# A hybrid layer: seven block products in two more phases of its first network, modulation weights in quarters, four modulation tiles on TensorE

## What is computed

```python
def swiglu(h, w_in, w_out):
    a, b = jnp.split(h @ w_in, 2, axis=-1)          # w_in 1024 x 5632
    return (jax.nn.silu(a) * b) @ w_out             # w_out 2816 x 1024

def trunk_layer(x, mod, n_pre, n_post, f_in, f_out, mix_w, ctx):
    sh0, sc0, g0, sh1, sc1, g1, sh2, sc2, g2 = jnp.split(mod, N_MOD, axis=-1)
    h = rms_norm(x, n_pre[0]) * (1 + sc0) + sh0
    x = x + 0.5 * g0 * rms_norm(swiglu(h, f_in[0], f_out[0]), n_post[0])
    h = rms_norm(x, n_pre[1]) * (1 + sc1) + sh1
    y, st = token_mixer(h, *mix_w, ctx)
    x = x + g1 * rms_norm(y, n_post[1])
    ...

mod_ctx = (jax.nn.silu(c_ctx) @ w_mod[l] + b_mod[l])[None, None, :]
mod_lat = (jax.nn.silu(c) @ w_mod[l] + b_mod[l])[:, None, :]
```

## Time and profile before

| | us |
|---|---|
| median of three runs | 1715.43 (1715.18 to 1716.39) |
| profiled execution, its own time | 1714.57 |
| its span | 1712.8 |
| TensorE busy | 1692.2, 99% |
| VectorE busy | 1031.9, 60% |
| ScalarE busy | 686.7, 40% |

### The profile page before, as it was taken

The page is one execution under the profiler, slowest core; times in us unless marked ns, Lnnn a source line. Parts: engine busy times, 40 slices in busy tenths (PEclk is TensorE's granted clock), DMA queues, the critical chain, the costliest instruction groups (busy, mean ns, idle before and its releaser), DMA issues.

```text
span 1712.8 us, 27981 instructions
## 1 busy us (share of the span) xinstructions
PE 1692.2 (99%) x11327; PEld 1561.5 (91%) x11327; DVE 1031.9 (60%) x1741; ACT 686.7 (40%) x1254; POOL 0.2 (0%) x4
## 2 busy tenths in 40 slices
PE   8999999999999999999999999999999999999998
PEld 6999899989979989999999889889889988998997
DVE  5756465666465323555537877774646834882785
ACT  6322222212365332343445555553464433551453
POOL 0000000000000000000000000000000000000000
PEclk9999999999999999999999999999999999999999
DMA  9435343433214224323343211111521222222233
GB/s 387 175 135 220 136 160 135 158 138 123 91 59 154 76 67 105 100 81 82 98 136 93 102 53 41 42 41 51 212 77 68 86 88 62 98 89 85 74 101 146
DMA packets 58650, 189.50 MB, mean 111 GB/s; under 512 B 7672, under 2 KB 16680, under 8 KB 56744
## 3 DMA queue, kind: packets, MB, share of 16 engines
q1 hardware_dynamic: 58536, 187.89, 32.5%
HBM read 170.67 MB, written 16.54 MB: 109 GB/s over the span
## 4 chain that ended last, share of the span: by engine, by line
PE 90%; DVE 4%; ACT 3%; issue 1%; DMA 1%; DVEq 0%; ACTq 0%; SPq 0%
PE psum L712 13%; PE psum L714 12%; PE psum L713 12%; PE psum L815 4%; PE psum L694 4%; PE psum L696 4%; PE psum L695 4%; PE psum L817 4%; PE psum L816 4%; PE psum L1236 2%; PE psum L1218 2%; PE psum L784 2%; PE psum L786 2%; PE psum L785 2%; PE psum L1196 2%; PE psum L1121 1%
## 5 line engine op out<-in xcount | busy, mean ns | idle before, releaser
L1870 DVE TENSOR_TENSOR wlo<-raw,whi 128x1024 fp32r<-128x1024 f32 x148 | 181.2, 1224 | 367.7 <-ACT whi L1330 367.7
L1330 ACT CAST whi<-raw 128x1024 fp32r<-128x1024 f32 x148 | 154.6, 1045 | 326.0 <-PE psum L817 140.8
L712 PE MATMUL psum<-h_hi,whi 128*128 128x320 f32 x720 | 223.8, 311 | 0.0
L714 PE MATMUL psum<-h_hi,wlo 128*128 128x320 f32 x720 | 222.5, 309 | 0.0
L713 PE MATMUL psum<-h_lo,whi 128*128 128x320 f32 x720 | 222.4, 309 | 0.0
L712 PE MATMUL psum<-g_hi,whi 128*128 128x320 f32 x656 | 209.4, 319 | 0.2 <-ACT gate L1688 0.2
L714 PE MATMUL psum<-g_hi,wlo 128*128 128x320 f32 x656 | 202.7, 309 | 0.0
L713 PE MATMUL psum<-g_lo,whi 128*128 128x320 f32 x656 | 202.6, 309 | 0.0
L712 PEld LDWEIGHTS psum<-h_hi,whi 128*128 128x128 f32 x720 | 135.1, 188 | 4.6 <-issue 4.5
L713 PEld LDWEIGHTS psum<-h_lo,whi 128*128 128x128 f32 x720 | 135.2, 188 | 0.0
L714 PEld LDWEIGHTS psum<-h_hi,wlo 128*128 128x128 f32 x720 | 135.1, 188 | 0.0
(11 more groups left out here) (440 smaller groups left out, 3707.3 us busy)
## 6 DMA issues: line engine op xcount, KB each, us to landing
raw<-in_w_ffn_in SPq DMA_DIRECT2D x88, 512.0 KB, 3.5
raw<-in_w_mix SPq DMA_DIRECT2D x77, 512.0 KB, 4.1
raw<-in_w_ffn_out SPq DMA_DIRECT2D x44, 512.0 KB, 3.5
mw<-in_w_mod SPq DMA_DIRECT2D x28, 768.0 KB, 5.1
mw<-in_w_mod SPq DMA_DIRECT2D x8, 1024.0 KB, 16.5
gate<-gate_keep SPq DMA_DIRECT2D x24, 320.0 KB, 4.7
mw<-in_w_mod SPq DMA_DIRECT2D x14, 512.0 KB, 4.5
gate_keep<-gate SPq DMA_DIRECT2D x20, 320.0 KB, 4.6
```

The lines of the kernel that those rows point to most:

```text
L712: mm(out, wh[:, k, :], hi[:, k, cols], start=(k == 0), stop=False)
L714: last = mm(out, wl[:, k, :], hi[:, k, cols], start=False, stop=(k == nk - 1))
L1330: copy((to or whi[t.slot])[:, :, :], raw[t.raw][:, :, :]).then_inc(w_hi, 1)
L1870: tt(lo[:, :, :], raw[t.raw][:, :, :], hi[:, :, :].bitcast(F32), ALU.subtract).then_inc(raw_free, 1)
```

## The change

- The pairs of the first network's phases two and three, 8 + 6 = 14, are made of seven products. Their token sums (ten differences and sums, four low parts) are made by VectorE in phase one, four high parts by ScalarE; each phase has its own PSUM banks so that bank 7 stays with the modulation.
- The modulation weights come in quarters of two blocks, 512 KB, into a ring of two places, in the order `MOD_ORDER`. Tiles 0 to 3 are multiplied by VectorE in phase one's in part, 4 to 6 in its out part, 11 to 13 in the out part of phase two (and 13's sum in phase three). Tiles 7 to 10 are multiplied by TensorE directly (`direct_mod`): one quarter behind the second and one behind the fifth product of each pair of phase two, with the conditioning vectors in a 32-column window of zeros as weights (`silc_win`).
- The sums of tiles 4 and 5, 11 and 12 stand in the middle of the out tiles v = 2 and v = 5, those of 6 and 13 behind the third product of the next phase. The turns of the result spread over pairs 1 to 4 of phase three.
- `x_tok` is loaded in two parts late: rows 0 and 1 behind the sixth product of the last pair, rows 2 to 4 behind the gain loads in the border. The tail of the constants (512 KB) is loaded during the mixers.
- The first network's six row tiles have homes of their own; three are split in the last pair, three behind its last product. Loops of the first network are written out.

The core of the diff:

```diff
-MOD_K = ((0, 3), (3, 6), (6, 8))
+MOD_PARTS, MOD_RING = 4, 2
+PART_K = KC // MOD_PARTS
+MOD_DIRECT = (7, 8, 9, 10)
+PAIR_PARTS = tuple(((n, part), (n, part + 1)) for n in MOD_DIRECT for part in (0, 2))
...
             def load_mod(n, part):
-                lo, hi = MOD_K[part]
-                if not (isinstance(n, int) and n == 0):
-                    sp.wait_ge(mod_mul, 2 * (KC * (n - 1) + hi))
...
+                where = MOD_ORDER.index((n, part))
+                if where >= MOD_RING:
+                    before = where - MOD_RING
+                    if MOD_ORDER[before][0] in MOD_DIRECT:
+                        sp.wait_ge(mod_pe, parts_until(before, True))
+                    else:
+                        sp.wait_ge(mod_mul, 2 * PART_K * parts_until(before, False))
...
+                        for n in SEVEN[1]:
+                            for one in PAIR_PARTS[n]:
+                                load_mod(*one)
+                            load_next(2 * n + 4)
+                            load_next(2 * n + 5)
...
-                    if f == 0 and p == 0:
-                        sp.wait_ge(pre_t, KC)
-                        sp.dma_start(x_tok[:, :, :].rearrange("p c d -> p (c d)"), a["x_tok"]).then_inc(x_back, 16)
...
+                        sp.wait_ge(tile_done, Tile(base + tiles - 2).n + 3)
+                        load_residual(a["x_tok"], slice(0, 2))
...
             mix(L_GATE, 2)
             load_post(0)
+            load_residual(a["x_tok"], slice(2, NT))
             mix(2, RAWS)
...
+                    if f == 0 and p == 1 and i in (1, 4):
+                        direct_mod(*PAIR_PARTS[n][i // 4])
+                    if f == 0 and i == 2:
+                        if p == 1 and n == 0:
+                            sum_mod(6)
+                        elif p == 2 and n == 0:
+                            sum_mod(13)
...
+            def direct_mod(n, part):
+                where = MOD_ORDER.index((n, part))
+                slot, skip = where % MOD_RING, 2 * (MOD_DIRECT[-1] - n)
+                if (n, part) == (MOD_DIRECT[0], 0):
+                    pe.wait_ge(cols_in, 4)
+                pe.wait_ge(mod_in[slot], 16 * (where // MOD_RING + 1))
+                for o in range(PART_K):
+                    k = part * PART_K + o
+                    for half in range(2):
+                        last = mm(mod_part(2 * (k % 2) + half, half), silc_win[:, k, skip:skip + MOD_COLS],
+                                  mw[:, slot * PART_K + o, half * MOD_HALF:(half + 1) * MOD_HALF], start=False, stop=False)
+                last.then_inc(mod_pe, 1)
...
-                    elif f == 1:
+                    else:
                         for n in SEVEN[p]:
-                            seven(SEVEN_FROM[p] + n, n, base)
...
+                            seven(f, p, n, base)
...
-                            out_tile(f, p, v, base, g_lo_s, NJ * f + j0)
-                            if f == 0 and v % 4 == 3:
-                                sum_mod(it + v // 4)
+                            mod = None
+                            if f == 0 and v in (2, 5):
+                                mod = (4, 11)[p] + v // 5
+                            out_tile(f, p, v, base, g_lo_s, NJ * f + j0, mod)
...
+                            elif f == 0:
+                                if v in (0, 1):
+                                    multiply(11, 2 * v)
+                                    multiply(11, 2 * v + 1)
+                                elif v == 4:
+                                    multiply(12, 2)
+                                    multiply(12, 3)
+                                elif v == 6:
+                                    multiply(13, 1)
+                                    multiply(13, 2)
```

More of the change, by code:

```diff
@@ L52 @@
 MOD_HALF = MOD_W // 2
-MOD_K = ((0, 3), (3, 6), (6, 8))
-FIRST_K = KC - MOD_K[0][1]
+MOD_PARTS, MOD_RING = 4, 2
+PART_K = KC // MOD_PARTS
+FIRST_K = KC - PART_K
+MOD_DIRECT = (7, 8, 9, 10)
+PAIR_PARTS = tuple(((n, part), (n, part + 1)) for n in MOD_DIRECT for part in (0, 2))
+MOD_ORDER = ([(n, part) for n in range(MOD_DIRECT[0]) for part in range(MOD_PARTS)]
+             + [one for pair in PAIR_PARTS for one in pair]
+             + [(n, part) for n in range(MOD_DIRECT[-1] + 1, MOD_LATER) for part in range(MOD_PARTS)])
+MOD_MULTIPLIED = [n for n in range(MOD_LATER) if n not in MOD_DIRECT]
+SILC_N = MOD_COLS + 2 * (len(MOD_DIRECT) - 1)
 RAWS = 4
@@ L369, in of_weights, with pair_banks, parts_until @@
             return w_sum[{1: 1, 3: 0, 4: 2, 5: 3}[i]][:, :, :]
-        def pair_banks(n):
-            return ((4, 5, 6), (0, 1, 7))[n % 2]
+        def pair_banks(f, p, n):
+            return SEVEN_BANKS[f][p][n % 2]
+        def parts_until(where, direct):
+            return sum((n in MOD_DIRECT) == direct for n, _ in MOD_ORDER[:where + 1])
         def pair_tiles(base, n):
@@ new lines, in ffn @@
+                    if f == 0 and p == 0:
+                        first_three()
+                        pe.wait_ge(pick_in, 2)
+                        pe.wait_ge(ld_cst, 16)
+                        pe.wait_ge(mod_ev, KC)
+                        for j in range(4):
+                            for half in (1 - j % 2, j % 2):
+                                last = mm(mod_part(j, half), pick_row[:, MOD_COLS:2 * MOD_COLS], cst[:, 0:MOD_HALF],
+                                          start=True, stop=(half != j % 2))
+                        last.then_inc(rows_zero, 1)
+                        tiles_in(0, 3)
+                        for n in range(nj // 2):
+                            if n:
+                                tiles_in(n)
+                            sum_mod(n)
+                    elif p == 0:
+                        first_four(1, base)
+                        tiles_in(0, 0, 4)
+                        for n in SEVEN[0]:
+                            seven(1, 0, n, base)
+                    else:
+                        for n in SEVEN[p]:
+                            seven(f, p, n, base)
@@ L2173, in scales, with over_k @@
                         per_group(V_POST + l * KC), ALU.mult, ALU.mult).then_inc(post_ready, 1)
-            def over_k(w, ks, done_mul, before):
-                for k in ks:
+            def over_k(n, part, ks):
+                where = MOD_ORDER.index((n, part))
+                slot, before = where % MOD_RING, 2 * KC * MOD_MULTIPLIED.index(n)
+                dve.wait_ge(mod_in[slot], 16 * (where // MOD_RING + 1))
+                for o in ks:
+                    k, w = part * PART_K + o, mw[:, slot * PART_K + o, :]
                     for g in range(2):
```

578 lines of the change are left out of this document (335 added, 243 removed).

## The result

The changed kernel takes **1718.85 us** (median of 11 runs, 1716.81 to 1721.84), the kernel before 1715.18 beside it. The ratio is 1.0021 (95% interval 1.0012 to 1.0030): 3.7 us slower by the medians, where 1710.6 was forecast, with a range that ended at 1719 and a chance of only 0.13 for slower.

The account below looks back on a forecast made before the run. TensorE, busy 99% of 1712.8 us, was taken as the bound. The profiled 1714.57 - 15.4 + 5.4 + 5.2 gave 1709.8; with the median's 0.86 more, 1710.6 us; 8-in-10 range 1702 to 1719.

Parts of the forecast that it names:

- Products and direct quarters: Phases two and three: seven products save 24.6 us, sixteen direct quarters add 12.2, four removed sums save 3.0; net -15.4.
- The edges: Either side of the narrow modulation matmuls: 0.3 of each quarter's 0.76 us, some 5 of the sixteen quarters' 12.2.
- The slack of 5 us: Steady pairs of phase two: direct quarters have some 5 us between landing and use, so cost nothing beyond 0.76 each.
- Waits in the out parts: TensorE waits 1.1 us at tile 5's sum, 1.9 at tile 12's, 2.3 at phase three's entry; together +5.4.
- 3.7 us of wait a us of landing: Out-part waits: each us of quarter landing beyond the assumed 3.8 adds about 3.7 us in all.
- The border: Late token load ahead of two mixer tiles brings the first normed row at +25.2 us instead of +20.0: +5.2 us.
- the stall at the fourth row tile: Border: TensorE wants the fourth tile at 4.1 us, its split ends at 6.45; 2.4 us, inside the border's +5.2.
- phase one's in part as covered: Phase one: added token work on VectorE fits beside eight-product tiles, thinly; if not, a pair loses up to 1 us.
- the sum of -4.8: Whole kernel: -15.4 for products and quarters, +5.4 for out-part waits, +5.2 for the border.
- The signs that the prediction gave for being right: Phase two about 111.4 us, phase three about 74, quarter groups 0.64, waits of 1 to 2 at sums, normed row about +25.
- Slower: Rival, chance 0.10: all quarters land in 6.3 us, out-part waits become 14.7 us, total 1719.9.

Follow-up runs that it names:

- s6: Changed kernel with three reorderings (first pair's quarter, out parts' VectorE work and loads, border's token load) and each pair's two direct quarters joined: 1700.4 us, ratio 0.9921.
- s3: Changed kernel with the 1.5 MB load of the last three token rows issued behind mixer tiles 2 and 3 instead of ahead: 1715.4 us.
- s1_start: Changed kernel with one modulation quarter of tile 0 moved behind the gate product that frees a bank in the first pair: 1716.9 us.
- a1: Changed kernel with four TensorE waits (sums of tiles 5 and 12, fourth row tile, first normed row) filled with four matmuls on constants each: 1717.8 us.
- b2: Kernel before, given a 2.62 us wait ahead of a phase-two modulation sum, that wait filled with five matmuls on constants: 1717.8 us, ratio 1.0014.
- s8: Same kernel as s6, with the stall at the fourth row tile filled with four matmuls: 1701.0 us against 1700.4.

## Why the prediction was wrong

Step by step:

- **Products and direct quarters**: forecast -15.4, measured -15.3 in the two stretches. The pitch of 0.147 us and 0.76 us a quarter held: 216.57 to 217.38 is 0.81 us in the changed kernel, again 0.66 over a pitch. The edges were as the rows had them, and s6 measured them apart: 0.33 us for one change there and back. The Trainium skill (TensorEngine Tiling (Array Packing), Tiling Modes) says that changing the tiling mode drains TensorE; the 0.33 us agrees with it, and no run separates a drain from other causes of the edge. The slack of 5 us that the prediction gave the quarters holds but for the first one, which waited for its load 0.5 to 1.3 us in three of the other executions (none in this one).
- **Waits in the out parts**: forecast 1.1, 1.9 and 2.3 (these add up to 5.3, where the prediction has 5.4), measured 1.90, 2.19 and 2.53, at those three places and no other. Quarters landed in a median of 4.1 and 4.3 us there, not 3.8: at 3.7 us of wait a us of landing that is 1.1 to 1.9 more, and 1.2 came.
- **The border**: first normed row forecast at +25.2 us, measured 25.05 (463.11 to 488.16); the stall at the fourth row tile forecast 2.4, measured 2.28. The last mixer tile's cast began at +21.5, forecast +21.7:

```profile
463.11 0.39 PE L891 MATMUL psum<-row_w,g_hi 128*128 128x512 f32 x1
...
484.65 1.05 ACT L1441 CAST first_w<-raw 128x1024 fp32r<-128x1024 f32 x1 [0.16 <-DMA raw<-in_w_mix]
```

  So the mixer tiles did come behind the 1.5 MB, and s3, which only exchanged the two, gave it back. The Trainium skill (DMA: Bandwidth & Descriptors, Queues, rings and completion order) says that each DMA engine consumes descriptors in ring order; the trace agrees, in that the 1.5 MB had landed at 482.1 us and the first of the two tiles was cast, as soon as it was there, at 483.44. It is not needed for the delay, though. SP issued the two tiles 11.7 us into the border here and 8.0 in s3 (whose border begins at 460.99), because issuing the 1.5 MB took SP 3.6 us; their casts then began 3.5 us apart. No run separates the two. The first line is the changed kernel's, the second s3's:

```profile
474.79 0.91 SPq L511 DMA_DIRECT2D raw<-in_w_mix  x2
469.01 4.64 SPq L511 DMA_DIRECT2D raw<-in_w_mix  x2
```

- **What failed** is the sum of the waits in the out parts. It let a wait cost its length. No row of the kernel before shows TensorE standing for 2 us after its start, nor the granted clock below 1.0, and the step had no term for what comes behind. Two of the four falls lay on the path, those behind the sums of tiles 5 and 12, 1.7 us each: 3.4. The fall behind the fourth row tile lay inside the wait for the normed row. That behind the normed row was taken up within the stage: from the row's turn to the second wait for `g_lo` it is 43.84 us before and 43.83 in the changed kernel. (The mean clock over the runs, 0.9988 to 0.9940, would be 8.2 us' worth if all of it lay on the path.) The first line is of the kernel before, the others of the changed one:

```profile
528.58 0.41 PE L886 MATMUL psum<-g_hi,whi 128*128 128x320 f32 x1 [1.23 <-DVE g_lo L2113]
...
488.16 1.97 PE L863 MATMUL psum<-cst,y 128*128 128x128 f32 x8 [2.27 <-DVE y L2267]
531.99 0.41 PE L1012 MATMUL psum<-g_hi,whi 128*128 128x320 f32 x1 [1.02 <-DVE g_lo L2272]
```

- **A place was left out**: the first pair of phase one. The prediction went through the out parts and the border, and costed phase one's in part as covered. It was, but the first pair's order on VectorE was not read: 2.3 us. A further 1.0 us lies ahead of it: TensorE, released by the constants' load, began at 4.34 us in this execution and at 3.69 in the one of before, and the work up to 16 us took 0.35 longer. The start varies: 3.47 to 3.69 in the three executions of the kernel before and its versions, 3.61 to 4.50 in the eleven of the changed one and its versions. Whether a part of that belongs to the change is not shown.

By spans of the two profiled executions the sum of -4.8 stands against +4.1. Of these 8.9 us the two falls are 3.4, the first pair 2.3, the longer waits 1.2, the part ahead of the first pair 1.0 and a rest behind the border 0.7, which no experiment followed up; that leaves 0.3. The signs that the prediction gave for being right all came, and the time was still missed, since they say nothing of what follows a wait. The rival *Slower* had the right sign for another reason: its quarters were to land in 6.3 us, and they landed in 4.1 to 4.4.

## What to carry to other kernels

A change that fills up an engine beside the bottleneck is judged by the order of that engine's work at each place where the bottleneck asks for it: here 15 us of saved matmuls were eaten by six waits of about 2 us and what follows them, and another order, with no work removed, made 3.7 us of loss into 10 us of gain (14 with joined quarters). Price a wait of TensorE of 2 us at its length plus up to 1.7 us, if nothing behind it waits anyway; here the 1.7 came behind about half of such waits. Where two waits stand one after the other and the second has an end of its own, shorten the chain to the second; filling or removing the first gave nothing here.

## What was not expected of the hardware

The granted clock falls behind a wait in some executions and not in others, at the same place: behind the sum of tile 5 in the profiled execution of the changed kernel (0.50 from 195 to 198 us), not in that of s1_start, where the wait was 2.08 us. So runs of one kernel spread: those of the changed kernel from 1716.8 at a mean clock of 0.995 to 1721.8 at 0.993. Five filled waits, a1's at the two sums and the fourth row tile, b2's and s8's, had at most 0.55 us left, and the profiles show no fall behind any of them.

Falls also came where TensorE had not stood, between 589 and 614 us, in twelve of the fourteen profiled executions, but not in those of the kernel before and of s6. Each began within 1.3 us of the end of 38 matmuls on blocks of 8 x 8 and 8 x 10, with which TensorE spends 2.9 us. In the changed kernel:

```profile
604.89 0.78 PE L1153 MATMUL psum<-cst,gi 8*128 8x8 f32 x10
...
606.76 1.09 PE L1157 MATMUL psum<-ar,sels 8*128 8x10 f32 x8
607.79 0.79 PE L1118 MATMUL psum<-whi,g_hi 128*128 128x512 f32 x1
```

So the clock did not fall only behind standing still: it fell behind a stretch of very small matmuls as well. No run took them away or filled them, so that they are the cause is not shown; the kernel before has the same 38.
